# A decoder step in one core: x loaded and split by token tiles of 96 rows of 8 KB

## The reference, cut to what matters

```
x = concat(x_prompt (512 tokens), x_sample (8 x 8 tokens))      # 576 tokens x 2048, float32
xn = x * rsqrt(mean(x*x, axis=-1) + 1e-6) * norm1_g
z  = xn @ w_in                                                  # 2048 x 6152 columns
# the last 8 columns of z are the input and forget gates of 4 mLSTM heads;
# the others feed a gated short convolution and the mLSTM (q, k, v, o)
x1 = x + concat(y_conv, y_mlstm) @ w_out
y  = rmsnorm(x1 + (silu(rms(x1) @ wg) * (rms(x1) @ wu)) @ wd)
```

## Time and profile before

| | us |
|---|---|
| median of three runs | 2488.28 (2487.45 to 2488.44) |
| the profiled execution | 2488.82, its span 2486.9 |
| TensorE busy in the span | 2464.2 (99%) |
| VectorE, ScalarE, GpSimd busy | 1766.2, 896.6, 38.3 |
| mean granted TensorE clock | 0.997 of full speed |
| first projection matmul starts | 33.76 |

### The profile page before, as it was taken

How to read it: one execution, slowest core, us unless ns; L and a number is a source line. 1 busy time by engine, 2 the same in 40 slices (tenths; PEclk the granted TensorE clock), 3 DMA queues, 4 the chain that set the end, 5 groups by cost and what they waited for, 6 DMA issues and landing times.

```text
span 2486.9 us, 44240 instructions
## 1 busy us (share of the span) xinstructions
PE 2464.2 (99%) x17592; PEld 2394.5 (96%) x17592; DVE 1766.2 (71%) x2482; ACT 896.6 (36%) x1236; POOL 38.3 (2%) x60
## 2 busy tenths in 40 slices
PE   8999999999999998999999999999999999999998
PEld 8999999999999997999999999999999899999886
DVE  7576575575687668787787778877777867766435
ACT  5212222122133335433444344433444533544413
POOL 0000000000000000000000000000000000000100
PEclk9999999999999999999999999999999999999999
DMA  5333233333235665343343434434333755755722
GB/s 131 96 120 98 78 116 103 89 105 98 86 115 155 188 194 195 112 127 115 106 127 110 130 108 118 127 111 127 101 104 109 249 155 149 269 137 146 275 81 76
DMA packets 458922, 325.53 MB, mean 131 GB/s; under 512 B 14130, under 2 KB 429006, under 8 KB 456368
## 3 DMA queue, kind: packets, MB, share of 16 engines
q1 hardware_dynamic: 403704, 250.29, 34.5%
q10 hardware_dynamic: 51448, 58.42, 7.7%
q0 software_dynamic: 3584, 14.16, 1.5%
HBM read 264.49 MB, written 58.34 MB: 130 GB/s over the span
## 4 chain that ended last, share of the span: by engine, by line
PE 60%; DVE 1%; ACT 0%; issue 0%; DVEq 0%; ACTq 0%
PE ps L844 17%; PE ps L848 17%; PE ps L846 17%; PE ps L859 2%; PE ps L961 2%; PE ps L963 2%; PE ps L965 2%; PE ps L921 1%; PE ps L988 0%; DVE oplo L2138 0%; PE ps L969 0%; PE ps L970 0%; PE ps L871 0%; PE ps L612 0%; DVE dwlo L2382 0%
## 5 line engine op out<-in xcount | busy, mean ns | idle before, releaser
L844 PE MATMUL ps<-ophi,gw_ring 128*128 128x288 f32 x3208 | 950.5, 296 | 4.0 <-DVE gw_ring L2125 4.0
L846 PE MATMUL ps<-oplo,gw_ring 128*128 128x288 f32 x3208 | 946.9, 295 | 0.0
L848 PE MATMUL ps<-ophi,gw_ring 128*128 128x288 f32 x3208 | 945.3, 295 | 0.0
L844 PEld LDWEIGHTS ps<-ophi,gw_ring 128*128 128x128 f32 x3208 | 602.3, 188 | 5.5 <-issue 4.5
L848 PEld LDWEIGHTS ps<-ophi,gw_ring 128*128 128x128 f32 x3208 | 604.8, 189 | 0.0
L846 PEld LDWEIGHTS ps<-oplo,gw_ring 128*128 128x128 f32 x3208 | 603.2, 188 | 0.1
L1044 ACT ACTIVATE whi<-wraw 128x512 fp32r<-128x512 f32 x256 | 160.9, 633 | 598.7 <-PE ps L607 425.4
L604 PE MATMUL ps<-xhi,whi 128*128 128x288 f32 x1536 | 333.1, 299 | 0.0
L604 PE MATMUL ps<-xlo,whi 128*128 128x288 f32 x1536 | 329.1, 296 | 0.0
L607 PE MATMUL ps<-xhi,wlo 128*128 128x288 f32 x1536 | 329.0, 296 | 0.0
L2125 DVE TENSOR_TENSOR gw_ring<-graw_a,gw_ring 128x1024 fp32r<-128x1024 f32 x191 | 233.9, 1224 | 112.2 <-ACT gw_ring L1291 111.5
(11 more groups left out here) (344 smaller groups left out, 2706.5 us busy)
## 6 DMA issues: line engine op xcount, KB each, us to landing
wraw<-in_w_in_dram SPq DMA_DIRECT2D x96, 512.0 KB, 3.9
graw_a<-in_w_ffn_gate_dram SPq DMA_DIRECT2D x59, 512.0 KB, 3.8
graw_a<-in_w_ffn_up_dram SPq DMA_DIRECT2D x59, 512.0 KB, 4.8
graw_a<-in_w_ffn_down_dram SPq DMA_DIRECT2D x42, 512.0 KB, 6.1
wraw<-in_w_out_dram SPq DMA_DIRECT2D x32, 512.0 KB, 4.1
opraw<-hop SPq DMA_DIRECT2D x14, 1152.0 KB, 10.9
graw_b<-in_w_ffn_gate_dram SPq DMA_DIRECT2D x29, 512.0 KB, 3.8
graw_b<-in_w_ffn_up_dram SPq DMA_DIRECT2D x29, 512.0 KB, 4.6
```

Source lines behind the costliest of these rows:

```text
L844: pe.matmul(out, gw_ring[:, slot, 0, k, :], ophi[p][:, k, :], start=start and k == 0, stop=False, skip_group_check=True)
L846: pe.matmul(out, gw_ring[:, slot, 0, k, :], oplo[p][:, k, :], start=False, stop=False, skip_group_check=True)
L848: mm = pe.matmul(out, gw_ring[:, slot, 1, k, :], ophi[p][:, k, :], start=False, stop=k == GK - 1, skip_group_check=True)
```

## The change: by token tiles instead of feature pieces

x is loaded token tile by token tile, whole rows of 8 KB. Tile 0 is sent at once; SP then waits until the gate weights have come (`gw_in`) before it issues tiles 1 to 4 and the two parts of tile 5. The work is cut in 12 units: unit n is half the features (8 blocks) of token tile n // 2. A unit is 8 transposes, one ScalarE copy and one VectorE subtraction of 768 columns each. The gate matmuls are no longer spread: `gates(a)` runs all 16 blocks for one half of the tokens, 32 matmuls in a row, the first after unit 8's transposes, the second after the last split. A token tile's square is one instruction over 2048 features: tiles 0 to 2 on ScalarE behind their splits, tile 3 on VectorE in the loop, tile 4 on VectorE after it, tile 5 after the gate columns are copied out. The turning of the identity matrix while pieces are awaited is gone (10 instead of 14 ahead of the first tile, none later). The weight quarters are split at n = 8 and 10. In the diff below the parts follow each other as SP, TensorE, ScalarE, VectorE. The other edits follow from the new counts of `tok_in`, and GpSimd's clearing of `qz` waits for `rb_rec` instead of the last transpose.

```diff
-    X_PIECES = ((0, 2), (2, 2), (4, 4), (8, 4), (12, 4))
+    XU = 2 * XT
+    KU = KT // 2
-    SQ_ACT = 4
-    IDLE_FIRST, IDLE_X, IDLE_PIECE = 6, 14, (2, 8)
+    SQ_ACT = 3
+    IDLE_FIRST, IDLE_X = 6, 10
...
-            for b, (k0, n) in enumerate(X_PIECES):
-                c = slice(k0 * P, (k0 + n) * P)
-                sp.dma_start(xtok[:, 0:XT - 1, c],
-                             xp[0:TP - last, c].rearrange("(t p) d -> p t d", p=XTW)).then_inc(tok_in[b], 16)
...
+            for t in range(XT - 1):
+                if t == 1:
+                    sp.wait_ge(gw_in, 16)
+                sp.dma_start(xtok[:, t, :], xp[t * XTW:(t + 1) * XTW, :]).then_inc(tok_in[t], 16)
+            sp.dma_start(xtok[0:last, XT - 1, :], xp[TP - last:TP, :]).then_inc(tok_in[XT - 1], 16)
+            sp.dma_start(xtok[last:XTW, XT - 1, :], xs[:, :]).then_inc(tok_in[XT - 1], 16)
...
+            def gates(a):
+                pe.wait_ge(x_lo, XU // 2 * (a + 1))
+                for k in range(KT):
+                    for moving in (xhi, xlo):
                         mm = pe.matmul(pair(0)[:, a, :], gw[:, k, :], moving[:, 2 * k + a, :],
                                        start=k == 0 and moving is xhi, stop=k == KT - 1 and moving is xlo)
+                    if k % KU == KU - 1:
+                        mm.then_inc(w_used, 1)
+            for n in range(XU):
+                t, kh = n // 2, n % 2
+                if n >= 3:
+                    pe.wait_ge(x_lo, n - 2)
+                if kh == 0:
+                    pe.wait_ge(tok_in[t], 16 if t < XT - 1 else 32)
+                for i in range(KU):
+                    k = kh * KU + i
+                    mm = pe.transpose(ps[:, 2 + 2 * (n % 3) + i // 4, (i % 4) * XTW:(i % 4 + 1) * XTW],
                                       xtok[:, t, k * P:(k + 1) * P], ident[0:XTW, 0:XTW])
                 mm.then_inc(xt_done, 1)
+                if n == XU - 4:
+                    pe.wait_ge(gw_lo, 2)
+                    gates(0)
+            gates(1)
...
+            for n in range(XU):
+                src, own = unit(n)
+                act.wait_ge(xt_done, n + 1)
+                act.activation(own(xhi), src, ACT.Copy).then_inc(x_hi, 1)
+                if n % 2 and n // 2 < SQ_ACT:
+                    square(n // 2)
+                if n in (8, 10):
+                    hi(1, (n - 8) // 2, gain=(n - 6) // 2)
...
+            for n in range(XU):
+                src, own = unit(n)
+                dve.wait_ge(x_hi, n + 1)
+                tt(own(xlo), src, own(xhi).bitcast(F32), ALU.subtract).then_inc(x_lo, 1)
+                if n == 2 * SQ_ACT + 1:
+                    square(SQ_ACT)
+                if n in (8, 10):
+                    split(1, (n - 8) // 2, V_G1)
+            square(XT - 2)
             tile_done(0)
             dve.tensor_copy(zg[:], pair(0)[0:4 * H]).then_inc(tile_read, 1)
+            link(square(XT - 1))
             split(1, 2, V_G1)
             split(1, 3, V_G1)
```

More of the change, by code:

```diff
@@ L185, in hybrid_trunk_step @@
         diag = take("diag", [XTW, XT, XTW])
-        ss_part = take("ss_part", [XTW, XT, len(X_PIECES)])
+        ss_part = take("ss_part", [XTW, XT, 1])
         zg = take("zg", [4 * H, 2, HT])
@@ L320, in hybrid_trunk_step @@
         tile_read = sem("tile_read")
-        tok_in = [sem(f"tok_in{b}") for b in range(len(X_PIECES))]
+        tok_in = [sem(f"tok_in{b}") for b in range(XT)]
         g1_in, gw_in, small_in = sem("g1_in"), sem("gw_in"), sem("small_in")
@@ L1051, in _, with square, unit @@
             act.activation(rstd_col[:, 0:1], ident[:, 0:1], ACT.Copy)
[L1052 removed]
+            act.wait_ge(gw_lo, 1)
             act.activation(gw[:, :, 0:2 * H], gw_raw[:], ACT.Copy).then_inc(gw_hi, 1)
[L1055 to L1074 removed]
+            def square(t):
+                x = xtok[:, t, :]
+                act.activation(x, x, ACT.Square, accum_out=ss_part[:, t, 0:1]).then_inc(ss_ok, 1)
+            def unit(n):
+                t, kh = n // 2, n % 2
+                cols = slice((t % 3) * XTW, (t % 3 + 1) * XTW)
+                own = lambda v: v.rearrange("p (h b k a) t -> p h b k a t", h=2, b=2, a=2)[:, kh, :, :, t // 3, cols]
+                bank = 2 + 2 * (n % 3)
+                return ps[:, bank:bank + 2, 0:4 * XTW].rearrange("p b (k t) -> p b k t", t=XTW), own
+            for n in range(XU):
[6 more added lines that the diff above has]
+                    hi(1, (n - 8) // 2, gain=(n - 6) // 2)
             hi(1, 2, gain=3)
@@ L1309, in operand_hi @@
             def operand_hi(j):
-                act.wait_ge(tok_in[j], 16 * 3 + 16)
+                act.wait_ge(tok_in[j], 16 * 2)
                 act.wait_ge(op_hi, j + 1)
@@ L1625, in _, with square, unit @@
             dve.memset(ssq_c[:], 0.0)
-            def square(b, t):
-                k0, n = X_PIECES[b]
-                x = xtok[:, t, k0 * P:(k0 + n) * P]
-                return stt(x, x, 1.0, x, ALU.mult, ALU.mult, accum_out=ss_part[:, t, b:b + 1])
-            squares = []
-            for k in range(KT):
-                p0 = 2 * (k % 3 + 1)
-                dve.wait_ge(x_hi, k + 1)
-                tt(xlo[:, 2 * k:2 * k + 2, :], ps[:, p0:p0 + 2, 0:HT],
-                   xhi[:, 2 * k:2 * k + 2, :].bitcast(F32), ALU.subtract).then_inc(x_lo, 1)
-                if k in X_LAST:
-                    squares += [(X_LAST[k], t) for t in range(SQ_ACT, XT)]
-                if squares and k % 2:
-                    square(*squares.pop(0))
-                if k in (KT - 4, KT - 2):
-                    split(1, (k - (KT - 4)) // 2, V_G1)
-            for b, t in squares:
-                ins = square(b, t)
-            link(ins)
+            def square(t):
+                x = xtok[:, t, :]
+                return stt(x, x, 1.0, x, ALU.mult, ALU.mult, accum_out=ss_part[:, t, 0:1])
+            def unit(n):
+                t, kh = n // 2, n % 2
+                cols = slice((t % 3) * XTW, (t % 3 + 1) * XTW)
+                own = lambda v: v.rearrange("p (h b k a) t -> p h b k a t", h=2, b=2, a=2)[:, kh, :, :, t // 3, cols]
+                bank = 2 + 2 * (n % 3)
+                return ps[:, bank:bank + 2, 0:4 * XTW].rearrange("p b (k t) -> p b k t", t=XTW), own
+            for n in range(XU):
[7 more added lines that the diff above has]
+            square(XT - 2)
             tile_done(0)
             dve.tensor_copy(zg[:], pair(0)[0:4 * H]).then_inc(tile_read, 1)
+            link(square(XT - 1))
             split(1, 2, V_G1)
             split(1, 3, V_G1)
-            dve.wait_ge(ss_ok, len(X_PIECES) * SQ_ACT)
+            dve.wait_ge(ss_ok, SQ_ACT)
             link(dve.tensor_reduce(ss_col[0:XTW, :], ss_part[:], mybir.AxisListType.X, ALU.add))
```

61 lines of the change are left out of this document (8 added, 53 removed).

## The result

| | median of the runs, us | range |
|---|---|---|
| before | 2487.95 | 2486.18 to 2489.05 (7 runs) |
| changed | 2497.63 | 2494.03 to 2500.82 (7 runs) |

The ratio is 1.0038, 95% interval [1.0029, 1.0048]: the change costs 9.7 us. The forecast was 2494.9 (+6.6) with a range of 2490.5 to 2497.5, both beside a median of 2488.3 before. The sign and the kind of the two costs were right; the time stands at the upper edge of the range, 0.1 us beyond it. The changed kernel also scatters more, 6.8 us against 2.9. Its profiled execution was the slowest of the seven (2500.82 us, span 2499.1, so 12.2 over the span of before); the same kernel profiled again (experiment 8) had a span of 2495.9 and took 2497.63 us, the median itself. Where the two profiles differ I give both, and the second is the typical one.

What follows compares the result with a forecast made beforehand. The prediction took TensorE, at work 99% of the span, as the bound. Tile 1's later start, +4.8 us, and the third stop's stall, +1.8, sum to +6.6 on 2488.3, so 2494.9 us, range 2490.5 to 2497.5.

Steps and rivals of the forecast that it cites:

- the two costs: A later start of tile 1's projections, +4.8 us, and a stall ahead of TensorE's third stop in tile 1, +1.8 us.
- Where the bound is: TensorE works 99% of the span; only tile 1's start and stops count, and delay at 60 us stands at the end.
- The gate weights, 6.5: At the start of the load: the gate weights land at 6.50 us, so SP sends tile 1 of x then.
- The rate of x, 239: Load of x: rows of 8 KB come at 239 GB/s, held there by the 96 partitions, not the row length.
- Landing, "Tile 4: 21.9": Load of x: tile 4's data end at 21.3 us, plus 0.6 until the waiting engine goes, so 21.9.
- Clock low for 3.4 us up to 25.3: TensorE from tile 4's landing at 21.9 us: low clock for 3.4 us, with 8.6 gate matmuls at the low pace.
- TensorE idle for 3.5 us for the last split: Ahead of the second 32 gate matmuls: TensorE stands 3.5 us, from 30.4, until VectorE's last split is done at 33.85.
- Stall of 1.8 ahead of the third stop: In tile 1: VectorE's longer queue starts the sum of squares 4.85 us after tile 1, so TensorE waits +1.8 us.
- What was put at 0: ScalarE's squares, tile 3's square on VectorE, later clearing of `qz`, fewer DMA issues on SP: no effect, 0 us.
- A: Rival at the start: the clock does not fall; +5.0 us with the second low stretch saved, +3.5 with both; chance 0.15.
- B: Rival in the load: x comes faster in rows of 8 KB, tile 4 3.8 us earlier, total +2.8 us; chance 0.20.
- C: Rival in the load: gate weights come late, their 32 B rows sharing DMA engines with 8 KB packets; +8.1 us; chance 0.10.

Runs made afterwards that it cites:

- experiment 8: The changed kernel unaltered, measured and profiled again: +9.5 us against before, ratio 1.0036.
- experiment 7: The changed kernel with the gate weights sent ahead of x on SP's own queue and no wait by SP: +4.7 us against before, ratio 1.0023.
- experiment 12: The changed kernel with the first five DMAs of x filling 128 partitions instead of 96, the extra rows unread: 2493.26 us, +5.3 against before (one run).
- experiment 4: The changed kernel with each run of 32 gate matmuls cut into two halves started earlier: +4.3 us against before, ratio 1.0018.
- experiment 2: The changed kernel with VectorE's square of tile 5 put ahead of the copy of the gate columns: +6.6 us against before, ratio 1.0027.
- experiments 1 and 3: The changed kernel without SP's wait for the gate weights, +20.2 us against before; the changed kernel with identity work in TensorE's gaps, +8.6 us.
- experiments 4 to 7 and 12: Those without their own line: changed kernel with gate matmuls halved, last square early, quarter 1 split late, +3.8 us against before; the same plus identity work, +4.0 us.
- experiment 11: The kernel before, with only the gate weights sent ahead of x on SP's queue: +2.3 us against before, ratio 1.0008 [0.9999, 1.0017].

## Why the prediction came out as it did

The forecast was +6.6 us and the medians give +9.7. By the second profile, whose execution took the median time, tile 1 costs 6.6 in place of 4.8 and the third stop 2.4 in place of 1.8, and the low clock behind that stop costs some 1.7, which the sum did not have. That is 10.7; 1.2 us come back at 950 to 1010 us, and the span ends 9.0 over the profile of before, which is itself 0.9 us over its median.

1. *Where the bound is.* Right: the difference arises before 70 us, at two places in TensorE's path, and stands in full up to 900 us. Not foreseen was that 1 to 1.6 us can change hands at 950 to 1010 us.
2. *The gate weights, 6.5.* 7.41 and 7.77 in the two profiles, late by 0.9 and 1.3, since a whole tile of 8 KB rows stood in the way (experiment 7).
3. *The rate of x, 239.* Right (229 to 246, and 238 to 283), and the reason given for it was right (experiment 12).
4. *Landing, "Tile 4: 21.9".* This step failed: 24.53, 2.6 late, and 23.24, 1.3 late. 0.9 and 1.3 of it are the gate weights. Tile 1 was worked out for 12.0 and came at 14.06 and 13.55, beyond the gate weights another 1.2 and 0.3: the allowance of 0.6 us from the last data to the waiting engine, taken from a 128-partition load, was too small by that much, and it varies from one execution to the next.
5. *Clock low for 3.4 us up to 25.3.* The mechanism was wrong. Without the identity work the clock was low long before tile 4 came (the transposes of tile 1 on already take 2.53 us). In the first profile it stayed low up to 31 us, and 22 in place of 8.6 gate matmuls paid 0.11 more each: +1.5. In the second it rose at 26.6 us, 9 gate matmuls paid, and the forecast's number came out by luck. Steps 4 and 5 give the 4.1 and 1.5 us by which tile 1 was late (43.73 and 41.16 against 39.65).
6. *TensorE idle for 3.5 us for the last split.* 3.7 in both. That quarter 1 ahead of split 11 and the wait for the last split cost here is shown by experiment 4; that gates(0) in a row ahead of unit 9 cost anything is not shown.
7. *Stall of 1.8 ahead of the third stop.* 2.3, since VectorE reached the sum of squares 5.3 us after tile 1 and not 4.85. Shown by experiment 2, with one thing missed: low clock behind the stall, +1.7, which the prediction did not consider. Both profiles of this kernel and those of experiments 1 and 3 have it; experiments 4 to 7 and 12, with waits of 1.9 to 2.35, do not, so the stall alone doesn't bring it, and what does stays open.
8. *What was put at 0.* That SP is ahead of the data no longer held: with the wait in its way DMA stood idle at 6 to 8 us, and taking that away (experiment 7) is worth 4.8 us in the median, 2.2 of them at tile 1. The squares on ScalarE were not tried alone; tile 2's transposes waited 0.85 us for VectorE's split in place of a DMA, so ScalarE and VectorE are no longer far from setting the pace there.
9. *The rivals.* A (the clock doesn't fall) and B (x faster) didn't happen. Experiment 12 makes B happen and is worth 4 us; that this is close to B's 3.8 is in part luck, since tile 1 gains 2.1 and the rest goes with the low clock that is absent behind the third stop. C's mechanism is real, and SP's wait is what prevents it.

## What to carry over

A wait that a change adds may be its best line: ask what it keeps apart before pricing it as a cost. A block of matmuls in an in-order queue costs what waits behind it; start each part as soon as its own inputs are there. Load small rows ahead on the queue of the large ones where that closes a gap in the DMA (where there is none, experiment 11, it gains nothing), and fill 128 partitions even with rows that nobody needs (one run). Before a difference of 2 us is put down to an edit, look where in the profile it arises and whether it still stands at the end.
